# A fused streaming-encoder layer: the opening reordered, the first block of each branch product split, and a store of the recurrent unit moved behind it

## The reference, cut to what matters

```
xn  = RMSNorm(x);  z = xn @ w_in
A   : 8 heads of forgetting attention, logit += c_t - c_s, c = cumsum(log sigmoid(f))
      the samples also see 256 cached keys, values and log forget values each
B   : width-4 causal conv -> gated linear recurrence h, 8 units of 128; y = gelu(lg) * h
C   : gated linear attention, 4 heads (d_k 128, d_v 256)
mix = (sum_b sigmoid(gate_b(xn)) * (y_b @ w_branch[b])) @ w_out
x   = x + RMSNorm(mix);  x = x + RMSNorm(relu(RMSNorm(x) @ w_up)^2 @ w_down)
```

## Time and profile before

| | us |
|---|---|
| median of 3 runs | 1577.84 |
| lowest, highest | 1577.53, 1578.05 |
| the profiled execution, whole | 1578.37 |
| its span, first to last instruction | 1576.6 |

### The profile page before, as it was taken

One profiled execution on the slowest core, in us unless ns is written; L12 is line 12 of the kernel. 1 busy time (PEld: TensorE's weight loads), 2 busy tenths in 40 slices (PEclk: granted clock), 3 DMA queues, 4 the chain that ended last, 5 costly groups with the idle time before them and its releaser, 6 DMA issues.

```text
span 1576.6 us, 26085 instructions
## 1 busy us (share of the span) xinstructions
PE 1508.9 (96%) x9854; PEld 1411.0 (89%) x9854; DVE 692.0 (44%) x1189; ACT 622.2 (39%) x1123; POOL 34.3 (2%) x39
## 2 busy tenths in 40 slices
PE   6799999999999989999999999997799999999996
PEld 6799999889999979998998899997798998998985
DVE  7355555532368762334445442333532322323234
ACT  6133333321277751244464432134451341431523
POOL 1000000000000000000000000001100000000003
PEclk9899999999999989999999999998799999999998
DMA  3976778222222212232332232521122222222222
GB/s 115 163 147 147 154 154 154 76 78 80 71 60 68 82 54 80 71 104 73 96 110 88 75 92 73 186 68 40 39 68 80 80 79 68 80 80 69 78 80 80
DMA packets 281350, 143.41 MB, mean 91 GB/s; under 512 B 73654, under 2 KB 268919, under 8 KB 281292
## 3 DMA queue, kind: packets, MB, share of 16 engines
q1 hardware_dynamic: 281300, 142.72, 34.5%
HBM read 129.86 MB, written 12.84 MB: 91 GB/s over the span
## 4 chain that ended last, share of the span: by engine, by line
PE 82%; DVE 8%; ACT 4%; issue 3%; DMA 1%; SPq 1%; DVEq 0%; ACTq 0%; POOL 0%
PE psum L564 45%; PE psum L940 14%; PE psum L955 14%; PE psum L658 1%; PE psum L688 1%; DMA w_raw<-in_w_in_dram 1%; DVE arena L1483 1%; DVE arena L1725 1%; ACT arena L1232 1%; DVE arena L1780 1%; PE psum L669 1%; PE psum L877 1%; PE psum L875 1%; PE psum L630 1%; ACT w_hi L1060 1%
## 5 line engine op out<-in xcount | busy, mean ns | idle before, releaser
L564 PE MATMUL psum<-XH,w_hi 128*128 128x320 f32 x1424 | 453.8, 319 | 6.5 <-DVE w_lo L1465 3.6
L564 PE MATMUL psum<-XH,w_lo 128*128 128x320 f32 x1424 | 443.6, 311 | 0.0
L564 PE MATMUL psum<-XL,w_hi 128*128 128x320 f32 x1424 | 443.4, 311 | 0.0
L1465 DVE TENSOR_TENSOR w_lo<-w_raw,w_hi 128x1024 fp32r<-128x1024 f32 x185 | 226.4, 1224 | 417.8 <-ACT w_hi L1060 417.0
L1060 ACT CAST w_hi<-w_raw 128x1024 fp32r<-128x1024 f32 x185 | 193.6, 1047 | 338.2 <-PE psum L955 166.3
L564 PEld LDWEIGHTS psum<-XH,w_hi 128*128 128x128 f32 x1424 | 270.9, 190 | 18.9 <-issue 9.8
L564 PEld LDWEIGHTS psum<-XL,w_hi 128*128 128x128 f32 x1424 | 270.9, 190 | 0.6
L564 PEld LDWEIGHTS psum<-XH,w_lo 128*128 128x128 f32 x1424 | 270.5, 190 | 0.0
L564 PE MATMUL psum<-YH,w_hi 128*128 128x320 f32 x512 | 160.4, 313 | 3.1 <-DVE YL L1859 2.0
L940 PE MATMUL psum<-XH,w_hi 128*128 128x320 f32 x512 | 159.1, 311 | 1.5 <-DVE fix L1929 1.5
L564 PE MATMUL psum<-YL,w_hi 128*128 128x320 f32 x512 | 159.6, 312 | 0.0
(11 more groups left out here) (254 smaller groups left out, 1748.7 us busy)
## 6 DMA issues: line engine op xcount, KB each, us to landing
w_raw<-in_w_in_dram SPq DMA_DIRECT2D x88, 512.0 KB, 3.7
w_raw<-in_w_up_dram SPq DMA_DIRECT2D x32, 512.0 KB, 4.0
w_raw<-in_w_down_dram SPq DMA_DIRECT2D x32, 512.0 KB, 3.5
w_raw<-in_w_branch_dram SPq DMA_DIRECT2D x24, 512.0 KB, 3.8
arena<-in_cache_fox_k_dram SPq DMA_DIRECT2D x32, 256.0 KB
arena<-in_cache_fox_v_dram SPq DMA_DIRECT2D x8, 1024.0 KB
out_dram<-arena SPq DMA_DIRECT2D x26, 256.0 KB, 2.5
arena<-in_state_gla_dram SPq DMA_DIRECT2D x4, 1024.0 KB, 5.4
```

The source lines that it names most:

```text
L564: mm = pe.matmul(Z[h][:, 0:HT], w[s][:, k, :], x[:, k, h * HT:(h + 1) * HT], start=(k == 0 and i == 0), stop=(k == KT - 1 and i == 2))
L1465: dve.tensor_tensor(WL[s][:, :, :], raw[s][:, :, :], WH[s][:, :, :].bitcast(F32), ALU.subtract).then_inc(w_lo, 1)
```

## The change

What it does, in the order of the program:

1. SP loads block 3, the keys of head 0 and block 4 ahead of the stores of the running sums; of the two stores the cached one goes first. The rest of the queue keeps its order.
2. PE makes the 16 transposes of the cached log forget values ahead of block 0, the banks in the order 4, 5, 2, 3, so that each waits only for the token tiles that used it. The transposes of the new log forget values and of their sums both stand between the two halves of block 2.
3. DVE negates the cached sums ahead of the scan of the new ones, and splits block 3 ahead of the copy of the turned values.
4. The first product block of each branch is `late_block`: k tiles 0 to 6 (0 to 5 for branch C) of both halves with a wait for the y of all heads but the last, then the remaining k tiles with the full wait. Three more blocks of each branch are written out, and the loop makes two rounds.
5. The tanh of block 58 stands ahead of the last cast to `YH` on ACT.
6. PE's transposes L775 stand behind the products of branch B, the copy to `LS` too; `LS` now lies in the tile of the gates, so the copy also waits for the last sum (`mix_sum`). Its four stores stand behind the loads of C's first head, and ACT waits for them after C's last head.

```diff
-        (WG, LG, GQ, TG, Y2, RA, RX, AA, TH, A2, MM, UU, HH, XC, XP, LS) = carve(
+        (WG, LG, GQ, TG, Y2, RA, RX, AA, TH, A2, MM, UU, HH, XC, XP) = carve(
...
+        LS = GT[:, :, :].rearrange("p a b -> p (a b)")[:, 0:D]
...
+        CP_ORD = (2, 3, 0, 1)
...
-            sp.wait_ge(ff_c, 1)
-            sp.dma_start(nc_new, ncT[0:FOX_HEADS, :]).then_inc(scr_out, 16)
-            sp.wait_ge(cp_scan, 1)
-            sp.dma_start(nc_past, cpast[0:FOX_HEADS, :].rearrange("h (b s) -> h b s", s=PAST)).then_inc(scr_out, 16)
             load(Lin(B_FOX + 2), (B_FOX + 2) % 2, w_fox(Lin(0), 2))
             for q in range(P // TB):
                 load_cache_k(slice(0, 1), 0, q)
+            load(Lin(B_FOX + 3), (B_FOX + 3) % 2, w_fox(Lin(1), 0))
+            sp.wait_ge(cp_scan, 1)
+            sp.dma_start(nc_past, cpast[0:FOX_HEADS, :].rearrange("h (b s) -> h b s", s=PAST)).then_inc(scr_out, 16)
+            sp.wait_ge(ff_c, 1)
+            sp.dma_start(nc_new, ncT[0:FOX_HEADS, :]).then_inc(scr_out, 16)
...
-            load(Lin(B_FOX + 3), (B_FOX + 3) % 2, w_fox(Lin(1), 0))
...
-            pe.wait_ge(nt_free, 2 * NT)
-            block(Lin(0), 0, XH, XL)
             pe.wait_ge(lfc_in, 16)
-            for r in range(16):
-                mm = pe.transpose(bank[2 + r // 4][0:FOX_HEADS, (r % 4) * P:(r % 4 + 1) * P],
-                                  cp_raw[:, r * FOX_HEADS:(r + 1) * FOX_HEADS], idf[:, :])
-                if r % 4 == 3:
-                    mm.then_inc(cp_pe, 1)
+            for j in CP_ORD:
+                pe.wait_ge(nt_free, 2 * NT if j < 2 else 2 * NT - 2)
+                for r in range(4 * j, 4 * j + 4):
+                    mm = pe.transpose(bank[2 + j][0:FOX_HEADS, (r % 4) * P:(r % 4 + 1) * P],
+                                      cp_raw[:, r * FOX_HEADS:(r + 1) * FOX_HEADS], idf[:, :])
+                mm.then_inc(cp_pe, 1)
...
+            block(Lin(0), 0, XH, XL)
             block(Lin(1), 1, XH, XL)
...
+            block(Lin(2), 0, XH, XL, (turn_lf, None))
             block(Lin(3), 1, XH, XL)
...
+            def late_block(b, s, y_sem, early, y_early, y_count):
+
+                pe.wait_ge(w_lo, (b + 1).v)
+                for ks in (range(early), range(early, KT)):
+                    pe.wait_ge(y_sem, y_count if ks.stop == KT else y_early)
+                    for h in range(2):
+                        if ks.start == 0:
+                            pe.wait_ge(z_free[h], b.v)
+                        for k in ks:
+                            for i, (w, x) in enumerate(((WH, YH), (WH, YL), (WL, YH))):
+                                mm = pe.matmul(Z[h][:, 0:HT], w[s][:, k, :], x[:, k, h * HT:(h + 1) * HT],
+                                               start=(k == 0 and i == 0), stop=(k == KT - 1 and i == 2))
+                        if ks.stop == KT:
+                            mm.then_inc(z_done[h], 1)
...
-                pe.wait_ge(y_sem, y_count)
-                with pe.Fori(0, KT // 2 - 1) as i:
+                late_block(Lin(B_MG[r] + 2), s, y_sem, early, y_early, y_count)
+                block(Lin(B_MG[r] + 3), 1 - s, XH, XL)
+                block(Lin(B_MG[r] + 4), s, YH, YL)
+                block(Lin(B_MG[r] + 5), 1 - s, XH, XL)
+                with pe.Fori(1, KT // 2 - 1) as i:
...
-            merge(0, y_done, 5 * FOX_HEADS)
+            merge(0, y_done, FOX_HEADS - 1, 5 * (FOX_HEADS - 1), 5 * FOX_HEADS)
...
+            merge(1, yl_done, LRU_N - 1, LRU_N - 1, LRU_N)
             pe.wait_ge(r_act, LRU_N)
             pe.wait_ge(last_dve, 1)
             for n in range(LRU_N):
                 mm = pe.transpose(bank[2 + n // 4][0:36, (n % 4) * P:(n % 4 + 1) * P], last[:, n, :], idf[:, :])
             mm.then_inc(last_pe, 1)
-            merge(1, yl_done, LRU_N)
...
+                if not cur:
+                    for h in range(2):
+                        gate(1, Lin(1), b + 1, 1, h)
...
-            for h in range(2):
-                gate(1, Lin(1), Lin(B_MG[1] + 1), 1, h)
+            merge(1)
             act.wait_ge(last_pe, 1)
+            act.wait_ge(mix_sum, 2 * KT)
             act.copy(LS[0:36, :], psum[0:36, 2:4, :].rearrange("p a b -> p (a b)")).then_inc(last_sb, 1)
-            merge(1)
...
-            step(dve.tensor_tensor_scan(c8, rn8, c8, 0.0, ALU.mult, ALU.add))
+            step(dve.tensor_scalar(cp8, cp8, -1.0, None, ALU.mult))
+            dve.tensor_tensor_scan(c8, rn8, c8, 0.0, ALU.mult, ALU.add).then_inc(cp_scan, 1)
+            dve.wait_ge(cp_scan, 1)
             dve.tensor_scalar(nc8, c8, -1.0, None, ALU.mult).then_inc(ff_c, 1)
-            dve.tensor_scalar(cp8, cp8, -1.0, None, ALU.mult).then_inc(cp_scan, 1)
+            lo(Lin(3), 1)
             dve.wait_ge(lfn_pe, 1)
             dve.tensor_copy(lfn[:, :, :], bank[6][:, 0:NT * 8].rearrange("p (t h) -> p t h", h=8)).then_inc(lfn_sb, 1)
-            lo(Lin(3), 1)
```

More of the change, by code:

```diff
@@ L469, in _ @@
             merge(1)
-            sp.wait_ge(last_sb, 1)
-            sp.dma_start(lc_p[0, 0], LS[0:3, :]).then_inc(stored, 16)
-            sp.dma_start(lc_s[0].rearrange("b j c -> (b j) c"), LS[3:27, :]).then_inc(stored, 16)
-            sp.dma_start(lh_p[0], LS[27:28, :]).then_inc(stored, 16)
-            sp.dma_start(lh_s[0], LS[28:36, :]).then_inc(stored, 16)
             load(Lin(B_GLA), B_GLA % 2, w_in_v[:, :, cgk:cgk + P])
-            sp.wait_ge(stored, 32 + 64)
+            sp.wait_ge(last_dve, 1)
             def gla_loads(h, first=False):
@@ L505, in _ @@
             gla_loads(Lin(0), True)
+            sp.wait_ge(last_sb, 1)
+            sp.dma_start(lc_p[0, 0], LS[0:3, :]).then_inc(stored, 16)
+            sp.dma_start(lc_s[0].rearrange("b j c -> (b j) c"), LS[3:27, :]).then_inc(stored, 16)
+            sp.dma_start(lh_p[0], LS[27:28, :]).then_inc(stored, 16)
+            sp.dma_start(lh_s[0], LS[28:36, :]).then_inc(stored, 16)
             with sp.Fori(0, GLA_H - 1) as i:
@@ L590, in _, with turn_lf @@
             mm.then_inc(col_pe, 1)
-            pe.wait_ge(nt_free, 2 * NT)
-            block(Lin(0), 0, XH, XL)
-            pe.wait_ge(lfc_in, 16)
-            for r in range(16):
-                mm = pe.transpose(bank[2 + r // 4][0:FOX_HEADS, (r % 4) * P:(r % 4 + 1) * P],
-                                  cp_raw[:, r * FOX_HEADS:(r + 1) * FOX_HEADS], idf[:, :])
-                if r % 4 == 3:
-                    mm.then_inc(cp_pe, 1)
-            block(Lin(1), 1, XH, XL)
-            pe.wait_ge(ff_lf, 1)
-            pe.wait_ge(col_sb, 1)
-            for t in range(NT):
-                mm = pe.transpose(bank[6][:, t * 8:t * 8 + 8], lfT[0:FOX_HEADS, tok(t)], idf[0:FOX_HEADS, 0:FOX_HEADS])
-            mm.then_inc(lfn_pe, 1)
-            block(Lin(2), 0, XH, XL)
-            pe.wait_ge(ff_c, 1)
-            for t in range(NT):
-                mm = pe.transpose(bank[7][:, t * 8:t * 8 + 8], cT[0:FOX_HEADS, tok(t)], idf[0:FOX_HEADS, 0:FOX_HEADS])
-            mm.then_inc(cn_pe, 1)
+            pe.wait_ge(lfc_in, 16)
+            for j in CP_ORD:
[4 more added lines that the diff above has]
+                mm.then_inc(cp_pe, 1)
+            def turn_lf():
+                pe.wait_ge(ff_lf, 1)
+                pe.wait_ge(col_sb, 1)
+                for t in range(NT):
+                    mm = pe.transpose(bank[6][:, t * 8:t * 8 + 8], lfT[0:FOX_HEADS, tok(t)], idf[0:FOX_HEADS, 0:FOX_HEADS])
+                mm.then_inc(lfn_pe, 1)
+                pe.wait_ge(ff_c, 1)
+                for t in range(NT):
+                    mm = pe.transpose(bank[7][:, t * 8:t * 8 + 8], cT[0:FOX_HEADS, tok(t)], idf[0:FOX_HEADS, 0:FOX_HEADS])
+                mm.then_inc(cn_pe, 1)
+            block(Lin(0), 0, XH, XL)
+            block(Lin(1), 1, XH, XL)
+            block(Lin(2), 0, XH, XL, (turn_lf, None))
             block(Lin(3), 1, XH, XL)
@@ L901, in _ @@
             merge_begin(2, (lambda: turn_o(Lin(GLA_H - 1)), None))
-            merge(2, gy_done, 2 * GLA_H)
+            merge(2, gy_done, 2 * (GLA_H - 1), 2 * (GLA_H - 1), 2 * GLA_H)
             def pairs(b0, n, AH, AL, a_ready=None):
@@ L1014, in _ @@
             pool.wait_ge(yl_done, LRU_N)
-            pool.wait_ge(stored, 32 + 64)
+            pool.wait_ge(last_dve, 1)
             pool.memset(QGB[:, :, :], 0.0)
@@ L1368, in _ @@
             act.wait_ge(gla_init, 1)
-            act.wait_ge(stored, 32 + 64)
             gla_head(Lin(0))
@@ L1372, in _ @@
                 gla_head(Lin(1, (1, i)))
+            act.wait_ge(stored, 32 + 64)
             gate(2, Lin(0), Lin(B_MG[2]), 0, 0)
@@ L1515, in _ @@
             cp8, lf8, fz8, c8, nc8, rn8 = (v[0:FOX_HEADS, :] for v in (cpast, lfT, fz, cT, ncT, rst_n))
-            for j in range(4):
-                dve.wait_ge(cp_pe, j + 1)
+            for n, j in enumerate(CP_ORD):
+                dve.wait_ge(cp_pe, n + 1)
                 ins_ = dve.tensor_copy(cp8.rearrange("h (q r) -> h r q", r=16)[:, 4 * j:4 * j + 4, :],
```

4 lines of the change are left out of this document (2 added, 2 removed).

## The result

| | before | after |
|---|---|---|
| median, us | 1577.68 | 1564.47 |
| lowest, highest | | 1564.0, 1565.17 |
| ratio after / before | | 0.9916, 95% interval 0.9899 to 0.9934 |
| the profiled execution, its span | 1578.37, 1576.6 | 1565.17, 1563.4 |

A forecast was written before the change was run, and what follows sets the result against it. PE holds 82% of the chain, so only its waits and slow stretches could go: opening 12.3, branch A 1.1, branch B 4.2, together 17.6 us off the median 1577.84, giving 1560.2; range 1555.5 to 1566.0.

The forecast's parts named there:

- rival B: Opening: store L417's 3.16 is its own, way to block 5's weights stays 12.2; gain 13.8, 1564.0; chance 0.19.
- PE and DVE in the opening: Opening: block 0 starts at 25.5, block 2 at 40.8, DVE's copy for the stores at 46.4, block 4 ends at 64.1.
- The values: SP's queue in the opening: stores out at 47.4, cached values issued at 49.2, 11.2 us earlier than before.
- The way to block 5's weights: SP's queue, from values issued to weights in: 11.1 us instead of 12.2, so weights at 60.3.
- From weights to block 5: Opening, cast, split, key transposes and two softmax tiles: 6.45 us, block 5 at 66.8, 12.3 earlier.
- The slow stretch after it: Block 5, behind PE's wait of some 2.5 us: PE runs slowly as before, no change charged.
- Branch A: First product of branch A: `late_block` covers the wait for the last `YL`, 1.1 us gained.
- Branch B: First product of branch B: starts 5.3 us earlier, at 574.4; net 4.2 after transposes and slow stretch, bounds 3.4 to 5.0.
- Branch C: First product of branch C: its y was ready already, so nothing gained.
- C: Opening: empty queue brings weights by 59, block 5 at PE's floor 65.3, no slow stretch; gain 21.3, 1556.5; chance 0.12.
- D: Twelve written-out blocks, four per branch: PE pauses for instructions, one 2.4 us pause each, 28.8 in all, 1589.0; chance 0.04.
- E: Opening: attention windows hang on DMA throughput, lead given back before head 2; 5.3 or less remains, 1572.5; chance 0.05.

The follow-up runs named there:

- the second execution: The changed kernel run again with no edit: 1565.05 us, ratio 0.9911.
- the branches alone: Kernel before with only the split products, earlier tanh and moved store, the opening as before: 1573.46 us, ratio 0.9973.
- the orders alone: Kernel before with only the PE and DVE orders in the opening changed, SP's queue as before: 1576.3 us, ratio 0.999.
- the keys late: Changed kernel with head 0's four key loads put back ahead of the stores of log forget values: 1569.75 us, ratio 0.9947.
- the two single undoings: Changed kernel with block 58's tanh back behind the last cast (1568.59 us) and, separately, with plain blocks in place of `late_block` (1568.41 us).

## Why the prediction was right or wrong, step by step

The time lies in the range and the direction was right, but the gain was put 4.4 us too high. The total of 13.2 is near rival B's 13.8, but by chance: B's late store did not come, and losses that B did not have made up for it.

**PE and DVE in the opening: right.** Block 0 started at 25.44 (25.5 foreseen), block 2 at 40.36 (40.8), the copy for the stores came at 45.65 (46.4), and block 4 ended on PE's own work.

**The values: right time by luck.** Forecast 49.2, measured 49.37: two errors cancelled. The last store was out at 46.80 instead of 47.4, but from there the stores took 2.57 to land and not 1.75. In the second execution it was more still.

**The way to block 5's weights: the term that failed.** I took 11.1, reasoning that block 4's weights ahead of the values had cost part of the 12.2. It measured 13.01, and in the other five executions with an empty queue ahead of the values and this order behind them it lay between 12.85 and 13.22. In the four kernels with something just ahead of the values it was no longer than that (12.27 before, 12.35 with the branches alone, 12.57 with the orders alone and with the keys late). The load ahead had cost nothing that shows, so an emptier queue could not give its time back; why the way is even a little longer behind an empty queue is open. What did cost was inside the stretch: the key quarter, 2.7 us in the one execution without it ahead of the weights. The rows for it were there (7.13 us for four key loads). This term is 1.9 of the shortfall. The estimate of 7.2 for the same way rested on a fit that the Trainium skill ("DMA: Bandwidth & Descriptors", Anatomy of one DMA) states for single DMAs issued by GpSimd, while these are six DMAs of SyncE; and the row set against it, 64.84 to 72.66, is a load that stood behind the values, so the 12.27 of the whole way was the number to set against it. Rival B had the way right.

**From weights to block 5:** 6.86 instead of 6.45. ACT's cast to DVE's last step took 5.83 in both kernels (72.66 to 78.49, and 62.38 to 68.21); the 0.4 is the five transposes ahead of block 5, 0.98 to its first matmul instead of 0.57, which now run slowly. With 0.2 from the values, block 5 came at 69.24 instead of 66.8, 2.4 late in all. PE's wait was 4.49 instead of 2.5.

**The slow stretch after it:** "runs slowly after it as before" was wrong by 0.6 (2.02 against 1.40 lost), besides those 0.4. The size does not follow from the opening's code: in the five executions with this opening and these loads the slow half took 5.53, 5.34, 4.24, 5.50 and 5.30. In the others with a wait of 2.7 us or more it was between 4.22 and 5.05.

**Branch A: right.** Forecast 1.1. The lead grew from 9.23 at the last transposes to 10.52 at the product, 1.3: the wait of 1.06, and 0.2 of hand-over around it. Put in its place again, the plain block waits 0.7 for `YL`. Its price was missed: 0.2 for `Z[0]` behind the split block, once in A and once in B; with another 0.3 that I could not place, 0.5 of the lead is gone by the last recurrent unit.

**Branch B: right.** Block 59 gained 5.27 (5.3 foreseen, wait 2.63 against 2.5), and 0.86 was paid back by branch C (0.8 to 1.0 foreseen for the transposes alone): the transposes took 0.87 and the `Z[0]` wait 0.2, and the slow stretch was 0.2 shorter than before. Net 4.4 against 4.2. Both ingredients were needed, as the two single undoings show.

**Branch C: right.** The lead is 14.42 ahead of it and 14.39 behind.

**The MLP: missed.** I assumed that PE's rate in the unchanged part stays. The group at the head of the MLP lost 1.1 to a longer slow stretch; what made it longer is open. The prediction's range allowed for the clock stretches at both ends, but its sum looked at the waits of the change only.

The sum of the misses: 2.4 (block 5) + 0.6 (its slow half) + 0.5 (small waits) + 1.1 (MLP) + 0.1 (small shifts in C and at the end) = 4.7, less 0.2 for branch A and 0.2 for branch B: 4.3, of 4.4.

**The rivals.** B: half right (the way did not shorten; it even came out at 13.0, not 12.2), half refuted (the store). C needed the weights earlier than the changed order brings them; its mechanism (block 5 at PE's floor and no slow stretch, 1556.5) was then reached by issuing the weights first, which gave 1558.0. D and E: refuted.

## What to carry to other kernels

When a queue is reordered to bring one load forward, add up what stands between its trigger and that load: loads in small pieces belong behind it, and a load that doesn't need the trigger belongs ahead of it (one load moved here, the weights issued ahead of the wait for the stores, was worth a further 6.5 us). Where a consumer waits for two things that come nearly together, freeing one alone brings little. A wait that goes on PE can take a slow stretch with it, but no fixed size should be put on that stretch: it cost 0.7 to 2.0 us behind block 5's wait, and nothing in the one execution where that wait was 1.81.

## What was not expected of the hardware

- The issue time of one and the same store was 0.39 to 0.51 us where the queue held no key loads ahead of it, and 1.92, 2.87, 3.01 and 3.16 where it did.
- The first 2 us after the queue had run empty moved 101 GB/s, the next 2 us 317.
- A wait of 1.81 (keys behind) was followed by no slow stretch in the next half block, one of 1.92 in the opening before by a granted clock of 0.50 from 45 to 48, and one of 2.63 ahead of block 59 by one that began late: PE's first matmuls after it, at 564.51, still ran at the full rate (0.39 listed for the first), and the granted clock fell behind them. With the branches alone and with the keys late the same wait was followed by slow matmuls at once (0.61 listed for the first). The windows of the changed kernel, columns as above:

```profile
564.00:566.00 2.00, 1.49 (x9) 1.52 (x10) 1.93 (x3) 0.69 (x2) 0.00 (x0) 0.86 0.01 3
566.00:568.00 2.00, 2.00 (x9) 2.00 (x9) 1.28 (x4) 1.57 (x2) 0.00 (x0) 0.50 0.00 0
```

- An unchanged group of 384 matmuls took between 57.89 and 59.32 us in thirteen executions.
